# Attention scores as three fp32r passes over split queries and keys, in a two-layer diffusion backbone on one Trainium2 core

## The chip, the cores and the metric

One core of one Trainium2 chip runs the whole kernel. The metric is device time in microseconds (us) for one execution. The kernel before was timed three times: 1687.32, 1690.92 and 1691.16 us, with a median of 1690.92 us.

## What is computed

A context stream of 256 tokens and a latent stream of 256 tokens, each 1024 wide, go through two layers. A layer is a half-step feed-forward (SwiGLU, hidden width 2816), a mixer, and a second half-step feed-forward. The mixer holds attention next to a gated convolution and a multi-scale pooling, and projects all three back. The part that the change touches is the score product of the differential attention:

```python
def _diff_attn(q, k, v, lam):
    s = jnp.einsum('bqhid,bkhid->bhiqk', q, k, preferred_element_type=jnp.float32)
    p = jax.nn.softmax(s * (ATTN_HEAD_DIM ** -0.5), axis=-1)
    a = p[:, :, 0] - lam * p[:, :, 1]
    return jnp.einsum('bhqk,bkhe->bqhe', a.astype(v.dtype), v)
...
    q = _apply_rope(_rms(q.reshape(B, S, H, 2, dh), q_norm_w), cos, sin)
    k = _apply_rope(_rms(k.reshape(B, S, H, 2, dh), k_norm_w), cos, sin)
    k_all = jnp.concatenate([k, kc], axis=1)
```

There are 4 heads with 2 branches of 64 dimensions each. In layer 0 the latent queries see all 512 keys and the context queries see the 256 context keys. In layer 1 the context stream gives keys and values only.

## The kernel before

The activations lie transposed: 128 features on the partitions, tokens along the free dimension, 512 tokens (T) for both streams and 256 (S) for the latent one alone. The weights come as a stream of 320 blocks of 128x1024 numbers. SyncE loads block after block into a ring of 5 (`raw`). For each block ScalarE (ACT) writes a rounded fp32r copy (`whi`, `split` at L426 to L433), and VectorE (DVE) writes the rest (`wlo = raw - whi`, L761). TensorE (PE) then multiplies in three fp32r passes, high by high, high by low, low by high (`three`, L1287 to L1291). A block is 24 such matmuls. Every engine runs a list of instructions in a fixed order, written out by hand; semaphores tie the lists together. ACT and DVE issue their halves of block n+4 at the point where PE works on block n.

The mixer of a layer (`mixer(l)` on each engine) first makes 4 key blocks (b = 0 to 3, 512 tokens wide) and 4 query blocks (b = 4 to 7, 512 wide in layer 0, 256 wide in layer 1). This is called the query/key stage here. For each block b:

- PE does the 24 matmuls of the block, and then `stat(b-1)` (L1542), an fp32 matmul that sums squares for the RMS norm. `stat(c)` waits for the squares of block c (`sqk_done`) and for the exponentials of blocks up to c-2 (`rq_done`).
- ACT, in the loop that starts at L580, splits the weights of block b+4, copies block b out of PSUM into `kq` (L583), squares it (L586), and calls `lnexp(b-1)`: a logarithm into `lnk` (L572) and an exponential into `rq` (L577), which is the inverse root of the mean square.
- DVE, in the loop at L1107, makes `wlo` of block b+4 and calls `rope(b-1)` (L1075 to L1086): the norm's multiplication (L1079, which waits for `rq_done`), a shuffle, two products with cosine and sine, and a sum back into `kq`, which counts `qk_ready`.

After the eighth block PE waits for the sixth exponential (`pe.wait_ge(rq_done, 8 * l + 6)`) and starts the four value blocks, since these write the PSUM banks that the norm sums of blocks 4 and 5 were in. In between come the last `stat`, then a wait for all eight `qk_ready`, and the first two score units.

The attention runs in units (`units(l)`): one tile of 128 queries and one head against 512 keys (8 units in each layer), and in layer 0 four more units with one context tile and two heads against 256 keys. `scores(k)` (L1578 to L1590) makes the scores of a unit: for each head the two branches lie on partitions 0 to 63 and 64 to 127, and each is one fp32 matmul with 64 rows of contraction, into a PSUM bank of its own:

```python
ins = pe.matmul(ps[:, 2 * (u % 2) + b, j * wk:(j + 1) * wk],
                kq[rows, H + hd, t * P:(t + 1) * P], kq[rows, hd, T - wk:T],
                start=True, stop=True)
```

The unit's maximum is taken on DVE (`unit_max`, L1123), the exponential on ACT (`unit_exp`, L603), the difference of the two branches on DVE (`unit_dif`, L1132 to L1144), the transposes on PE (`turn`, L1602) and the product with the values on PE (`values`, L1620). Units 0 and 1 have their scores among the value blocks. The others are interleaved with 16 half blocks of the convolution and pooling projections, one unit for each half block. This is called the unit stage here.

Of the kernel before, what the change touches and what calls it, by code (L numbers as in the profile page):

```python
# [26 lines left out]
P = 128  # L27
# [7 lines left out]
H = 4  # L35
# [71 lines left out]
def program(nc, wstream, wmod, cols, x_t, out):  # L107
    with ExitStack() as ctx:
# [25 lines left out]

        shared_a = sb("shared_a", [P, 3 * T])
# [25 lines left out]
        wm0_place.close()  # L161
        kq = sb("kq", [P, 8, T])
        vt = sb("vt", [P, 4, T])
        cx = sb("cx", [P, 8, T])
# [67 lines left out]
        qk_ready = sem("qk_ready")  # L232
        score_done = sem("score_done")
# [32 lines left out]


# [48 lines left out]
        def ntile(l):  # L316
            return T if l == 0 else S
# [107 lines left out]
        def _(act):  # L425
# [134 lines left out]
            def mixer(l):  # L560
# [18 lines left out]

                for b in range(QKB):  # L580
                    split_next(n0 + b)
                    act.wait_ge(block_done, n0 + b + 1)
                    act.activation(kq[:, b, 0:wid(b)], ps[:, b % 4, 0:wid(b)], ACT.Copy).then_inc(evac, 1)  # L583
                    if b >= 2:
                        act.wait_ge(qk_stat, 8 * l + b - 1)
                    act.activation(sqk[:, b % 2, 0:wid(b)], ps[:, b % 4, 0:wid(b)], ACT.Square)\  # L586
                        .then_inc(sqk_done, 1)
                    if b >= 1:
                        lnexp(b - 1)
# [65 lines left out]
                split_next(n0 + VQ)  # L655
                lnexp(QKB - 1)
                split_next(n0 + VQ + 1)
                unit_exp(0)
# [90 lines left out]
        def _(dve):  # L749
# [337 lines left out]

            def lambda_sums():
# [17 lines left out]
            def mixer(l):  # L1106
                n0, w = B_win[l], ntile(l)  # L1107
                for b in range(QKB + 1):
                    split_next(n0 + b)
                    if b >= 1:  # L1110
                        rope(l, b - 1)

# [57 lines left out]
                split_next(n0 + VQ + 1)  # L1170
                unit_max(0)
# [114 lines left out]
        def _(pe):  # L1286
# [251 lines left out]
            def mixer(l):  # L1538
# [38 lines left out]
                def scores(k):  # L1577
# [4 lines left out]
                    if k >= 2:  # L1582

                        pe.wait_ge(exp_done, u - 1)
                    for j, hd in enumerate(hds):
                        for b in range(2):
                            rows = slice(DH * b, DH * b + DH)
                            ins = pe.matmul(ps[:, 2 * (u % 2) + b, j * wk:(j + 1) * wk],  # L1588
                                            kq[rows, H + hd, t * P:(t + 1) * P], kq[rows, hd, T - wk:T],
                                            start=True, stop=True)  # L1590
# [86 lines left out]
                pe.wait_ge(qk_ready, 8 * (l + 1))  # L1677
# [151 lines left out]
```

## Time and profile before

| what | value |
|---|---|
| median of three runs | 1690.92 us |
| the profiled execution's own time | 1691.61 us |
| its span | 1689.6 us |
| mean granted TensorE clock | 0.996 of full speed |
| TensorE busy (matmuls) | 1670.4 us, 99% |
| VectorE busy | 1099.2 us, 65% |
| ScalarE busy | 616.1 us, 36% |
| chain that ended last, by engine | PE 95%, DVE 2%, ACT 1%, issue 1%, DMA 1% |
| score matmuls (L1588) in that chain | 1% of the span |
| layer 0: query/key stage and value blocks | about 427 to 490 us from the span's start |
| layer 0: unit stage | about 490 to 560 us |
| layer 1: query/key stage | about 1376 to 1398 us |
| layer 1: value blocks, then unit stage | 1398 to 1424 us, then to about 1475 us |

A timeline row gives the start in us from the span's start, the length in us, the engine, the line, the operation, what is written and read, the shape and the number of instructions that were merged into the row. The last bracket, if there is one, is how long the engine had been idle and what ended that. PEld is TensorE's weight load, which can run beside its matmuls. An fp32 matmul of the program shows as two weight loads and two matmul records. The length of a record is longer than the distance to the next one on the same engine, since instructions overlap: the distance between starts is what an instruction costs in a dense stretch.

### The profile page before, as it was taken

To read this page: it belongs to the slowest core of one execution; us is meant where nothing else is said; L and a number is where in the kernel's file an instruction comes from. 1 tells how busy PE (TensorE), PEld (TensorE's weight loads), DVE (VectorE), ACT (ScalarE), POOL (GpSimd) and SP (SyncE) were. 2 spreads that over 40 slices of the span, in tenths; PEclk is the share of its full clock that TensorE was granted. 3 is DMA by queue.
4 is the path that set the end of the run, shared out by engine and by line. 5 is a ranking of instruction groups with operands and counts; after the bars stand their busy time and mean duration, and the time that the engine had idled before them with its cause. 6 is when DMAs were issued, how large, how long until landed. Compare 5 with 4: busy or idle time off the path is not lost.

```text
span 1689.6 us, 23906 instructions
## 1 busy us (share of the span) xinstructions
PE 1670.4 (99%) x9501; PEld 1411.1 (84%) x9501; DVE 1099.2 (65%) x1681; ACT 616.1 (36%) x948; POOL 84.7 (5%) x150
## 2 busy tenths in 40 slices
PE   7999999999999999999999999999999999999999
PEld 3788888889777898888878898888888897899999
DVE  4777777636668567787773377777723377876654
ACT  4422222124545443222222252222222265565542
POOL 0000000000000100101000000000000000100000
PEclk8999999999999999999999999999999999999999
DMA  9355555532211224555553224555422232255554
GB/s 370 116 190 181 195 179 192 182 112 76 94 68 51 80 86 159 181 193 184 190 176 124 87 101 162 192 183 191 158 100 93 81 110 91 89 189 186 179 183 150
DMA packets 69466, 249.42 MB, mean 148 GB/s; under 512 B 7536, under 2 KB 8560, under 8 KB 69360
## 3 DMA queue, kind: packets, MB, share of 16 engines
q1 hardware_dynamic: 50928, 180.82, 30.8%
q0 software_dynamic: 18432, 67.12, 11.8%
q8 instruction: 75, 1.23, 0.3%
q14 instruction: 31, 0.25, 0.0%
HBM read 246.86 MB, written 1.05 MB: 147 GB/s over the span
## 4 chain that ended last, share of the span: by engine, by line
PE 95%; DVE 2%; ACT 1%; issue 1%; DMA 1%; POOL 0%; POOLq 0%; ACTq 0%; DVEq 0%
PE ps L1289 30%; PE ps L1290 29%; PE ps L1291 29%; PE ps L1448 1%; PE ps L1588 1%; PE ps L1620 1%; PE ps L1548 1%; PE ps L1396 1%; ACT whi L432 0%; PE ps L1602 0%; DMA raw<-wstream 0%; DVE wlo L761 0%; PE ps L1424 0%; DVE nmax L1123 0%; PE ps L1463 0%
## 5 line engine op out<-in xcount | busy, mean ns | idle before, releaser
L761 DVE TENSOR_TENSOR wlo<-raw,whi 128x1024 fp32r<-128x1024 f32 x320 | 393.0, 1228 | 498.0 <-ACT whi L432 497.1
L432 ACT ACTIVATE whi<-raw 128x1024 fp32r<-128x1024 f32 x320 | 338.5, 1058 | 847.2 <-PE ps L1291 754.6
L1289 PE MATMUL ps<-xh,whi 128*128 128x512 f32 (+1 forms) x1580 | 585.9, 371 | 4.8 <-issue 2.0
L1290 PE MATMUL ps<-xl,whi 128*128 128x512 f32 (+1 forms) x1580 | 569.3, 360 | 0.0
L1291 PE MATMUL ps<-xh,wlo 128*128 128x512 f32 (+1 forms) x1580 | 568.8, 360 | 0.0
L1289 PEld LDWEIGHTS ps<-xh,whi 128*128 128x128 f32 x1580 | 298.3, 189 | 63.9 <-issue 16.7
L1290 PEld LDWEIGHTS ps<-xl,whi 128*128 128x128 f32 x1580 | 298.7, 189 | 46.8 <-issue 3.8
L1291 PEld LDWEIGHTS ps<-xh,wlo 128*128 128x128 f32 x1580 | 298.5, 189 | 45.3
L1289 PE MATMUL ps<-ah,whi 128*128 128x512 f32 (+2 forms) x976 | 324.3, 332 | 1.1 <-DVE shared_b L809 1.0
L1291 PE MATMUL ps<-ah,wlo 128*128 128x512 f32 (+2 forms) x976 | 322.2, 330 | 0.0
L786 DVE SCALAR_TENSOR_TENSOR shared_a<-wm,cs,shared_a 128x512 f32<-128x512 f32 x448 | 307.5, 745 | 0.0
L1290 PE MATMUL ps<-al,whi 128*128 128x512 f32 (+1 forms) x800 | 272.3, 340 | 0.0
L1289 PEld LDWEIGHTS ps<-ah,whi 128*128 128x128 f32 x976 | 184.8, 189 | 20.8 <-DVE shared_b L809 2.3
L1291 PEld LDWEIGHTS ps<-ah,wlo 128*128 128x128 f32 x976 | 184.9, 189 | 17.0
L1290 PEld LDWEIGHTS ps<-al,whi 128*128 128x128 f32 x800 | 151.7, 190 | 16.6
L390 POOL DMA_DIRECT2D wm<-wmod x126 | 66.5, 528 | 872.7 <-DVEq L789 865.1
L1290 PE MATMUL ps<-ah,whi 128*128 128x258 f32 x352 | 99.7, 283 | 0.0
L1290 PEld LDWEIGHTS ps<-ah,whi 128*128 128x128 f32 x352 | 66.9, 190 | 0.0
L828 DVE SCALAR_TENSOR_TENSOR h<-ps,gcol,h 128x256 f32<-128x256 f32 x104 | 45.6, 477 | 22.8 <-PE ps L1291 22.7
L522 ACT ACTIVATE shared_a<-h 128x256 f32<-128x256 f32 (+1 forms) x64 | 31.4, 496 | 62.5 <-DVE h L828 59.9
L1289 PE MATMUL ps<-al,whi 128*128 128x256 f32 x176 | 49.8, 283 | 0.0
L1291 PE MATMUL ps<-al,wlo 128*128 128x256 f32 x176 | 49.8, 283 | 0.0
(128 smaller groups left out, 1106.1 us busy)
## 6 DMA issues: line engine op xcount, KB each, us to landing
raw<-wstream SPq DMA_DIRECT2D x320, 512.0 KB, 3.5
wm<-wmod POOLq DMA_DIRECT2D x128, 512.0 KB, 4.6
wm<-wmod SPq DMA_DIRECT2D x8, 1024.0 KB, 17.6
h<-x_t SPq DMA_DIRECT2D x4, 512.0 KB, 6.6
out_t<-h SPq DMA_DIRECT2D x8, 128.0 KB, 2.6
K<-cols SPq DMA_DIRECT2D x1, 939.0 KB, 20.1
K<-cols SPq DMA_DIRECT2D x1, 265.5 KB, 2.7
lamk<-cols SPq DMA_DIRECT2D x1, 256.0 KB, 16.5
```

Of the source, the lines that this page charges most:

```text
L390: pool.dma_start(wm[:, c, :, :].rearrange("p a n -> p (a n)"), wmod[bass.ds(i * 2 + c, 1)].rearrange("a p n -> p (a n)"))\
L432: act.activation(whi[:, n % SPL, :, :].rearrange("p a b -> p (a b)"), raw[:, n % RING, :], ACT.Copy)\
L522: act.activation(sq[:, d % 2, a:b], h[:, d, a:b], ACT.Square).then_inc(sq_done, 1)
L761: dve.tensor_tensor(wlo[:, n % RING, :, :].rearrange("p a b -> p (a b)"), raw[:, n % RING, :], whi[:, n % SPL, :, :].rearrange("p a b -> p ...
L786: ins = dve.scalar_tensor_tensor(acc, src, sc, acc, ALU.mult, ALU.add)
L828: ins = dve.scalar_tensor_tensor(h[:, d, v * S:(v + 1) * S], ps[:, bank, v * S:(v + 1) * S], gcol[:, m, d, v:v + 1], h[:, d, v * S:(v + 1) ...
L1289: pe.matmul(out_ap, hi_w, hi_x, start=start, stop=False)
L1290: pe.matmul(out_ap, hi_w, lo_x, start=False, stop=False)
L1291: return pe.matmul(out_ap, lo_w, hi_x, start=False, stop=stop)
L1396: ins = pe.matmul(ps[32 * g:32 * g + 2, ROWS_BANKS[d % 2], 0:w], cs[:, 2 * c:2 * c + 2], wm0[:, d, c // 4, g * w:(g + 1) * w], start=c < 4 ...
L1448: ins = pe.matmul(ps[32 * j:32 * j + 32, ROWS_BANK, 0:P], col("pick", 31 - r, 32), macc[:, v, j * P:(j + 1) * P], start=r == 0, stop=u + 1 ...
L1548: pe.matmul(ps[:, stat_bank(b), 0:wb], col("halves", 0, P), sqk[:, b % 2, 0:wb], start=True, stop=True)\
```

## The change

The scores are no longer fp32 products. After `rope(b)`, ACT writes a rounded fp32r copy of `kq[:, b]` (`head_high`), and DVE overwrites `kq[:, b]` with the rest (`head_low`; `kql` is the same memory as `kq`, with the type fp32r). The copies lie in memory that is free in this stage: `kh` and `qh` over `shared_a` and `shared_b`, the last one over a part of `cx`. Each score product becomes three fp32r matmuls that add up in PSUM. The wait of PE for all eight `qk_ready` goes away; instead `scores` waits for the low half of its own query head, and the first one also for the last logarithm.

```diff
--- before.py
+++ after.py
@@ -132,6 +132,10 @@
         qws = sb("qws", [P, 16])
         mrows = sb("mrows", [P, P])
 
+        heads = ExitStack()
+        qh = heads.enter_context(nc.sbuf_tensor("qh", [P, 3, T], F32R))
+        kh = heads.enter_context(nc.sbuf_tensor("kh", [P, 4, T], F32R))
+        heads.close()
         shared_a = sb("shared_a", [P, 3 * T])
         macc = shared_a[:, 0:2 * HN].rearrange("p (v n) -> p v n", v=2)
         sq = shared_a[:, 0:2 * T].rearrange("p (a t) -> p a t", a=2)
@@ -159,8 +163,15 @@
         lamk = wm0_place.enter_context(nc.sbuf_tensor("lamk", [P, NLAM], F32))
         lamt = wm0_place.enter_context(nc.sbuf_tensor("lamt", [P, 2, DH], F32))
         wm0_place.close()
+        heads_low = ExitStack()
+        kql = heads_low.enter_context(nc.sbuf_tensor("kql", [P, 8, T], F32R))
+        heads_low.close()
         kq = sb("kq", [P, 8, T])
         vt = sb("vt", [P, 4, T])
+        fifth = ExitStack()
+        fifth.enter_context(nc.sbuf_tensor("five", [P, 5, T], F32))
+        qh_last = fifth.enter_context(nc.sbuf_tensor("qh_last", [P, T], F32R))
+        fifth.close()
         cx = sb("cx", [P, 8, T])
         sqk = sb("sqk", [P, 2, T])
         lnk = sb("lnk", [P, T])
@@ -230,6 +241,8 @@
         rq_done = sem("rq_done")
         qk_used = sem("qk_used")
         qk_ready = sem("qk_ready")
+        kq_hi = sem("kq_hi")
+        kq_lo = sem("kq_lo")
         score_done = sem("score_done")
         max_done = sem("max_done")
         exp_done = sem("exp_done")
@@ -265,6 +278,9 @@
         srow_done = sem("srow_done")
 
 
+        def kq_high(b):
+            return kh[:, b, :] if b < 4 else qh[:, b - 4, :] if b < 7 else qh_last[:, :]
+
         def width(m):
             return T if m < 5 else S
 
@@ -577,6 +593,11 @@
                     act.activation(rq[:, c % 2, 0:wid(c)], lnk[:, 0:wid(c)], ACT.Exp, scale=-0.5)\
                         .then_inc(rq_done, 1)
 
+                def head_high(b):
+
+                    act.wait_ge(qk_ready, 8 * l + b + 1)
+                    act.activation(kq_high(b)[:, 0:wid(b)], kq[:, b, 0:wid(b)], ACT.Copy).then_inc(kq_hi, 1)
+
                 for b in range(QKB):
                     split_next(n0 + b)
                     act.wait_ge(block_done, n0 + b + 1)
@@ -585,6 +606,8 @@
                         act.wait_ge(qk_stat, 8 * l + b - 1)
                     act.activation(sqk[:, b % 2, 0:wid(b)], ps[:, b % 4, 0:wid(b)], ACT.Square)\
                         .then_inc(sqk_done, 1)
+                    if b >= 2:
+                        head_high(b - 2)
                     if b >= 1:
                         lnexp(b - 1)
 
@@ -653,8 +676,10 @@
                     act.activation(xh[:, 0:H, t * P:(t + 1) * P], of[:, t, :, :], ACT.Copy).then_inc(yh_done, 1)
 
                 split_next(n0 + VQ)
+                head_high(QKB - 2)
                 lnexp(QKB - 1)
                 split_next(n0 + VQ + 1)
+                head_high(QKB - 1)
                 unit_exp(0)
                 split_next(n0 + VQ + 2)
                 unit_exp(1)
@@ -1085,6 +1110,13 @@
                 own(dve.tensor_tensor(rot[:, :], shf[:, :], col("sin", 0, S), ALU.mult))
                 dve.tensor_tensor(kq[:, b, 0:S], kq[:, b, 0:S], rot[:, :], ALU.add).then_inc(qk_ready, 1)
 
+            def head_low(l, b):
+
+                wb = T if b < 4 else ntile(l)
+                dve.wait_ge(kq_hi, 8 * l + b + 1)
+                dve.tensor_tensor(kql[:, b, 0:wb], kq[:, b, 0:wb], kq_high(b)[:, 0:wb].bitcast(F32),
+                                  ALU.subtract).then_inc(kq_lo, 1)
+
             def lambda_sums():
 
                 for l in range(DEPTH):
@@ -1109,6 +1141,8 @@
                     split_next(n0 + b)
                     if b >= 1:
                         rope(l, b - 1)
+                    if b >= 2:
+                        head_low(l, b - 2)
 
                 us = units(l)
 
@@ -1168,6 +1202,7 @@
                         .then_inc(yl_done, 1)
 
                 split_next(n0 + VQ + 1)
+                head_low(l, QKB - 1)
                 unit_max(0)
                 split_next(n0 + VQ + 2)
                 unit_max(1)
@@ -1582,12 +1617,19 @@
                     if k >= 2:
 
                         pe.wait_ge(exp_done, u - 1)
+                    if k == 0:
+
+                        pe.wait_ge(lnk_done, 8 * (l + 1))
+                    pe.wait_ge(kq_lo, 8 * l + H + hds[-1] + 1)
                     for j, hd in enumerate(hds):
-                        for b in range(2):
-                            rows = slice(DH * b, DH * b + DH)
-                            ins = pe.matmul(ps[:, 2 * (u % 2) + b, j * wk:(j + 1) * wk],
-                                            kq[rows, H + hd, t * P:(t + 1) * P], kq[rows, hd, T - wk:T],
-                                            start=True, stop=True)
+                        q_hi, k_hi = kq_high(H + hd), kq_high(hd)
+                        q_lo, k_lo = kql[:, H + hd, :], kql[:, hd, :]
+                        for i, (q, k_) in enumerate(((q_hi, k_hi), (q_hi, k_lo), (q_lo, k_hi))):
+                            for b in range(2):
+                                rows = slice(DH * b, DH * b + DH)
+                                ins = pe.matmul(ps[:, 2 * (u % 2) + b, j * wk:(j + 1) * wk],
+                                                q[rows, t * P:(t + 1) * P], k_[rows, T - wk:T],
+                                                start=i == 0, stop=i == 2)
                     ins.then_inc(score_done, 1)
 
                 def turn(k):
@@ -1674,7 +1716,6 @@
                 value_block(0)
                 stat(QKB - 1)
                 value_block(1)
-                pe.wait_ge(qk_ready, 8 * (l + 1))
                 scores(0)
                 value_block(2)
                 scores(1)
```

The instruction lists show where the new operations stand. In each list L-numbers are those of that version. First ScalarE in the query/key stage of layer 1, at b = 4, before:

```order
L432 ACTIVATE whi<-raw 128x1024 [waits block_done,raw_in4]
L583 ACTIVATE kq<-ps 128x256 [waits block_done]
L586 ACTIVATE sqk<-ps 128x256 [waits qk_stat]
L572 ACTIVATE lnk<-ps,K 128x512 [waits rq_done,qk_stat]
L577 ACTIVATE rq<-lnk 128x512 [waits qk_used,lnk_done]
```

and after the change (`kh<-kq` is `head_high`):

```order
L448 ACTIVATE whi<-raw 128x1024 [waits block_done,raw_in4]
L604 ACTIVATE kq<-ps 128x256 [waits block_done]
L607 ACTIVATE sqk<-ps 128x256 [waits qk_stat]
L599 ACTIVATE kh<-kq 128x512 [waits qk_ready]
L588 ACTIVATE lnk<-ps,K 128x512 [waits rq_done,qk_stat]
L593 ACTIVATE rq<-lnk 128x512 [waits qk_used,lnk_done]
```

Between the square of block b and the logarithm of block b-1 there is now a copy of block b-2, which waits for `qk_ready`, the end of DVE's `rope(b-2)`. The logarithm behind it waits with it.

Then VectorE in the same stage, at b = 3, before:

```order
L761 TENSOR_TENSOR wlo<-raw,whi 128x1024 [waits hi_done]
L1079 SCALAR_TENSOR_TENSOR kq<-kq,K,rq 128x512 [waits rq_done]
L1083 STREAM_SHUFFLE shf<-kq 128x256 [waits qk_used]
L1084 TENSOR_TENSOR kq<-kq,K 128x256 [waits dve_step]
L1085 TENSOR_TENSOR rot<-shf,K 128x256
L1086 TENSOR_TENSOR kq<-kq,rot 128x256 [waits dve_step]
```

and after the change (`kql<-kq,kh` is `head_low`):

```order
L786 TENSOR_TENSOR wlo<-raw,whi 128x1024 [waits hi_done]
L1104 SCALAR_TENSOR_TENSOR kq<-kq,K,rq 128x512 [waits rq_done]
L1108 STREAM_SHUFFLE shf<-kq 128x256 [waits qk_used]
L1109 TENSOR_TENSOR kq<-kq,K 128x256 [waits dve_step]
L1110 TENSOR_TENSOR rot<-shf,K 128x256
L1111 TENSOR_TENSOR kq<-kq,rot 128x256 [waits dve_step]
L1117 TENSOR_TENSOR kql<-kq,kh 128x512 [waits kq_hi]
```

The subtraction of block b-2 now stands between the sum that ends `rope(b-1)` and the next weights.

Last, TensorE at the second score unit of layer 0, at the end of a value block and the start of the next, before:

```order
L1291 MATMUL ps<-whi,xl 128x512
L1588 MATMUL ps<-kq 128x512 x2
L1289 MATMUL ps<-whi,xh 128x512 [waits lo_done]
L1290 MATMUL ps<-wlo,xh 128x512
L1291 MATMUL ps<-whi,xl 128x512
```

and after the change:

```order
L1326 MATMUL ps<-whi,xl 128x512
L1630 MATMUL ps<-kh,qh 128x512 [waits kq_lo]
L1630 MATMUL ps<-kh,qh 128x512
L1630 MATMUL ps<-kql,qh 128x512 x2
L1630 MATMUL ps<-kh,kql 128x512 x2
L1324 MATMUL ps<-whi,xh 128x512 [waits lo_done]
L1325 MATMUL ps<-wlo,xh 128x512
L1326 MATMUL ps<-whi,xl 128x512
```

Two fp32 matmuls became six fp32r matmuls, in three pairs; the two of a pair use partitions 0 to 63 and 64 to 127.

## Rows read from the trace of the kernel before

**Rows 1.** Waits of TensorE over the whole span: total us, times, longest us.

```profile
PE ps L1620 <- DVE of L1154: 1.7, 1, 1.7
```

**Rows 2.** Timeline, first score unit of layer 0: start us, length us.

```profile
475.08 0.30 PEld L1588 LDWEIGHTS ps<-kq 64*128 64x128 f32 x4 [0.35 <-issue]
475.08 0.70 PE L1588 MATMUL ps<-kq 64*128 64x512 f32 x2
...
475.08 1.13 PE L1588 MATMUL ps<-kq 64*128 64x512 f32 x4
476.14 0.50 PE L1289 MATMUL ps<-whi,xh 128*128 128x512 f32 x1
```

**Rows 3.** Timeline, first unit of layer 0 with two heads (TensorE).

```profile
518.99 0.49 PE L1588 MATMUL ps<-kq 64*128 64x256 f32 x2
...
518.99 0.70 PE L1588 MATMUL ps<-kq 64*128 64x256 f32 x4
...
520.05 0.33 PE L1602 MATMUL ps<-K,att 128*128 128x128 f32 x1
```

**Rows 4.** Timeline, TensorE, last key and query blocks of layer 1.

```profile
1394.75 0.59 PE L1548 MATMUL ps<-sqk,K 128*128 128x256 f32 x2
...
1398.05 0.59 PE L1548 MATMUL ps<-sqk,K 128*128 128x256 f32 x2
1398.29 0.58 PE L1289 MATMUL ps<-whi,xh 128*128 128x512 f32 x1
...
1409.95 0.70 PE L1588 MATMUL ps<-kq 64*128 64x512 f32 x2
```

**Rows 5.** Timeline, ScalarE (ACT), query/key stage of layer 1.

```profile
1386.39 0.58 ACT L583 ACTIVATE kq<-ps 128x512 f32<-128x512 f32 x1
...
1387.35 0.69 ACT L572 ACTIVATE lnk<-ps,K 128x512 f32<-128x512 f32 x1
1388.07 0.63 ACT L577 ACTIVATE rq<-lnk 128x512 f32<-128x512 f32 x1
1388.60 1.04 ACT L432 ACTIVATE whi<-raw 128x1024 fp32r<-128x1024 f32 x1
1389.55 0.36 ACT L583 ACTIVATE kq<-ps 128x256 f32<-128x256 f32 x1
...
1396.62 0.48 ACT L572 ACTIVATE lnk<-ps,K 128x256 f32<-128x256 f32 x1
1397.13 0.42 ACT L577 ACTIVATE rq<-lnk 128x256 f32<-128x256 f32 x1
```

**Rows 6.** Timeline, VectorE (DVE), the same stage.

```profile
1385.58 0.75 DVE L1079 SCALAR_TENSOR_TENSOR kq<-kq,K,rq 128x512 f32<-128x512 f32 x1 [1.34 <-ACT rq L577]
...
1387.99 1.22 DVE L761 TENSOR_TENSOR wlo<-raw,whi 128x1024 fp32r<-128x1024 f32 x1
1389.12 0.75 DVE L1079 SCALAR_TENSOR_TENSOR kq<-kq,K,rq 128x512 f32<-128x512 f32 x1
...
1396.20 0.48 DVE L1079 SCALAR_TENSOR_TENSOR kq<-kq,qws,rq 128x256 f32<-128x256 f32 x1
...
1398.34 1.22 DVE L761 TENSOR_TENSOR wlo<-raw,whi 128x1024 fp32r<-128x1024 f32 x1
```

**Rows 7.** Groups by form that stand nearest to the added operations.

```profile
L817 DVE TENSOR_TENSOR al<-shared_b,ah 128x512 fp32r<-128x512 f32 x66 | 45.2, 684 | 1.0 <-ACT ah L451 0.7
...
L451 ACT ACTIVATE ah<-shared_b 128x512 fp32r<-128x512 f32 x66 | 40.6, 615 | 4.2 <-DVE shared_b L809 4.2
...
L817 DVE TENSOR_TENSOR al<-shared_b,al 128x256 fp32r<-128x256 f32 x22 | 9.2, 419 | 0.5 <-ACT al L451 0.5
L451 ACT ACTIVATE al<-shared_b 128x256 fp32r<-128x256 f32 x22 | 8.9, 403 | 1.4 <-DVE shared_b L997 1.3
```

**Rows 8.** Waits of VectorE from 1424 to 1448 us.

```profile
DVE nmax L1123 <- PE ps L1588: 2.8, 1, 2.8
```

**Rows 9.** Layer 1 stretches; PE, PEld, DVE, ACT, POOL busy us, then granted clock.

```profile
1448.00:1475.00 27.00, 24.80 (x196) 23.41 (x195) 21.77 (x37) 16.19 (x30) 4.27 (x4) 1.00 0.30 102
```

## The prediction

> **What bounds the kernel now.** I read the waits of TensorE (PE) first. Over the whole span it waits for other engines in very few places; the largest is 1.7 us for VectorE (DVE) in the unit stage of layer 1 [rows 1], and none lies in the mixer of layer 0. So nearly every us that PE's own work gains or loses in the mixer of layer 0 moves the end one for one, and work on ScalarE (ACT) and DVE is free as long as PE does not come to wait for it. Then I read the timeline of the score units, to price a score product, and last the timelines of the query/key stage of layer 1, where PE's steps are shortest and the other two engines have the least room. A change of 0.3%, about 5 us here, is about what a measurement of this kernel can tell from no change.
>
> **Score units on PE.** An fp32 matmul is two records. In the first unit of layer 0 the first pair of records (one for each branch) ends 0.70 us after the start, both pairs end after 1.13 us: one step is 0.43 us for 512 columns, and the two branches run side by side on their halves of the partitions, since two records share one step [rows 2]. The next work starts 1.06 us after the unit's start [rows 2], so the unit is 2 x 0.43 plus 0.20 us for getting in and out. A unit with two heads, 256 columns, ends its first pair after 0.49 us and its second after 0.70: a step of 0.21 us, four of them and the same 0.2 make the 1.06 us from 518.99 to 520.05 [rows 3].
>
> What does an fp32r pair cost? No row shows one with 64 rows of contraction. The fp32 step of 256 columns streams each column twice in its 0.21 us, as much as one fp32r pass over 512 columns would; and its pair of weight loads is as large as the new one and is hidden under that step, since the steps come 0.21 us apart [rows 3]. So I take 0.21 us for a pair of 512 and, for a pair of 256, half a step, 0.11 us. A 512 unit becomes 3 x 0.21 + 0.20 = 0.83 us, 0.23 less than 1.06; I take 0.21 less, for a little more per instruction. A two-head unit becomes 6 x 0.11 + 0.20 = 0.86 us; I take 0.15 less than 1.06, since its weight loads have only half as long to hide in. The bounds: nothing is gained if the loads are not hidden, and 0.4 us per unit is lost if the branches do not run side by side (both under the rivals).
>
> Which units count? In layer 0 all: 8 x 0.21 + 4 x 0.15 = 2.3 us. In layer 1 the first three: scores 0, 1 and 2 are in the path, and at unit 2 DVE waits 2.8 us for PE [rows 8]. From there on DVE has no other wait for PE until 1448 us [rows 8], and it is PE that then waits 1.7 us for DVE [rows 1]. A faster PE only waits longer there, so units 3 to 7 gain nothing. That is 3 x 0.21 = 0.6 us. Sum of the gain: 2.9 us.
>
> **New work on ACT and DVE: 16 copies and 16 subtractions.** The nearest forms are the same operations on the hidden values: copy 615 ns at 512 and 403 ns at 256 columns, subtraction 684 and 419 ns [rows 7]. On both engines the next instruction starts some 0.1 us before the record of the last one ends (in rows 5 the copy and the square of 0.58 and 0.59 us take 0.96 us together; in rows 6 the 1.22 us weight subtraction at 1387.99 is followed at 1389.12). So I charge 0.51 and 0.30 us for a copy, 0.59 and 0.34 for a subtraction.
>
> In layer 0 all eight blocks are 512 wide, PE takes over 6 us for each (24 matmuls of about 0.23 and a norm sum), and what ACT and DVE add, 1.1 us a block, has its cover. The same holds for the value blocks, 5.83 us each (two of them lie between 1398.29 and 1409.95) [rows 4].
>
> In layer 1 a query block is 256 wide and a block with its norm sum takes 3.30 us (1394.75 to 1398.05) [rows 4]. DVE needs 1.13 + 2.14 = 3.27 us for each (the weight subtraction, and the rope from 1396.20 to 1398.34) [rows 6]; it had no room. Worse, a ring of waits now ties the two engines: the logarithm of block b-1 stands behind the copy of b-2, which waits for the end of rope(b-2), and rope(b-1) waits for the exponential. Step by step, with a rope of 512 columns 2.41 us (1385.58 to 1387.99) and ready 0.08 later, of 256 columns 2.14 and 0.08 [rows 6]; logarithm and exponential of 512 together 1.25 us to the next instruction (1387.35 to 1388.60), of 256 about 0.84, and the exponential's end 0.09 later [rows 5]:
>
> - rope(1) is ready at 1388.07, as before. The copy of block 1 runs to 1388.6; before, the logarithm of block 2 began at 1387.35. Its exponential ends at 1390.0, and rope(2) starts there, not at 1389.12.
> - rope(2) is ready at 1392.5, the copy ends at 1393.0, the exponential of block 3 at 1394.4, rope(3) starts there and is ready at 1396.9. DVE meanwhile does the subtractions.
> - ACT ends that round at 1394.3. Its split (0.94 us) and the copy of block 5 (0.27) then put the square of block 5 at 1395.5 to 1395.9. PE wanted it at 1394.75 for its norm sum [rows 4]: **1.2 us of waiting**.
> - The copy of block 3 starts at 1397.0, the exponential of block 4 ends at 1398.4. DVE, with low(2) (0.59) and the weights (1.13) behind rope(3), starts rope(4) at 1398.6 (before 1396.20 [rows 6]), ready at 1400.8.
> - The next split puts the square of block 6 at 1399.5 to 1399.9; PE, shifted by 1.2, wanted it at 1399.25: **0.7 us more**.
> - The copy of block 4 (0.30) starts at 1400.8, the exponential of block 5 ends at 1402.1, where it ended at 1397.55 [rows 5]. The first value block waits for it. It started at 1398.29 [rows 4] and now starts at 1402.1: **1.9 us more**, 3.85 us in all.
>
> Behind it nothing adds: the value blocks give both engines 5.83 us each. By the same steps the last rope is ready at 1412.5 and the first unit's maximum starts 0.3 us later than PE's shift explains, with a value block between it and the next score that waits for it. The first score needs the last logarithm (about 1409.8) and low(4) (1405), and comes at 1413.8. PE's shift stays: DVE's chain from unit 2 on is released by PE [rows 8].
>
> The price of the stall has its ends too. It is nothing if the rounds overlap better than I have them, and if each added operation of blocks 0 to 5 stood in the path it would be 4 x (0.51 + 0.59) + 2 x (0.30 + 0.34) = 5.7 us. I take the worked-out 3.85, from the rows at the place itself.
>
> **Sum.** 1691.61 (the profiled execution) + 3.85 - 2.9 = 1692.5 us. The median of the runs shown is 1690.92, 0.7 below the profiled one. The forecast is no change that can be told.
>
> **The rivals.**
>
> Loads that are not hidden. If each new pair shows its weight loads, a pair costs more by half of the 0.20 us of getting in and out [rows 2], 0.10 us. A 512 unit is then 3 x 0.21 + 0.20 + 2 x 0.10 = 1.03 us, no gain worth naming, and a two-head unit 6 x 0.11 + 0.20 + 5 x 0.10 = 1.36, 0.30 more: 3.85 - 0.3 + 1.2 = 4.7, so 1696.3 us. It decides from 0.05 us a pair. Against it speak the 0.21 us steps of [rows 3], where loads into the same rows were hidden. The Trainium skill ("TensorE: Matmul & The Clock Gate", Part 3: Packing small matmuls) says that a weight load overlaps a running matmul only where the row group differs; by that rule it would come out as this rival, and the rows disagree with it for fp32. Chance 0.08.
>
> Branches that do not run side by side (**slower**). Then a 512 unit has six passes of 0.21 and costs 1.46, 0.4 more, and a two-head unit 12 x 0.11 + 0.20 = 1.52, 0.46 more: 11 x 0.4 + 4 x 0.46 = 6.2 us, and 0.3 more in layer 1 where five units lose 2.0 us and only 1.7 is spare. With the stall 10.4: 1702.0 us. Against it: the shared steps of [rows 2]. For it: no fp32r pair is in the trace. It decides once a pair takes over 0.30 us. Chance 0.12.
>
> A stall that costs more: PE idle for 3.85 us within 8, and the granted clock, 1.00 also where PE was busy 24.8 of 27 us [rows 9], falls to the lower level. If the first value block ran at 1.2 GHz in place of 2.4, it would take up to 5.8 us more, so 1698.3 us. Chance 0.09. Against it: the stall comes in three parts with norm sums and a query block between them.
>
> No stall: ACT and DVE keep up after all. Then 1691.61 - 2.9 = 1688.7 us. It wants an ACT round that doesn't wait for rope. The order of the lists speaks against it. Chance 0.13. That the products stay fp32 is ruled out by the types in the list of the changed program; that they gain far more than 0.21 has no source, 0.03.
>
> **How the numbers follow.** The forecast has a chance of 0.55, with 1690.5 to 1695 as its own range, for stalls of 2 to 6 us. The range takes in the case without a stall, the loads that are not hidden and the loss of the clock: 1688.3 to 1698.3, and leaves out mainly the branches one after the other. Faster by over 0.3% (under 1685.9) takes more than all the gains together: 0.04. Slower by over 0.3% (over 1696.0) is 0.12 from the branches, 0.05 from the loads and 0.07 from the clock: 0.24. Within 0.3%: 0.72.
>
> **What the next profile would show.** Right: PE waits for a square (ACT) before the norm sums of blocks 5 and 6 of layer 1, and for an exponential before the first value block, 3 to 5 us together; score units of about 0.85 us; the wait for the attention output (L1154 in the version before) grown from 1.7 to some 2.7 us; nothing new in layer 0. Wrong: score units over 1.06 us, a value block in layer 1 that starts on time, or a granted clock of half after 1395 us.

## The result, and the profile after the change

| | before | after |
|---|---|---|
| median | 1690.01 us (18 runs, 1685.18 to 1692.07) | 1692.62 us (18 runs, 1689.90 to 1695.70) |
| profiled execution: span | 1689.6 us | 1693.5 us |
| profiled execution: mean granted clock | 0.996 | 0.995 |

The ratio is 1.0018, with a 95% interval from 1.0011 to 1.0025: some 3 us slower, within the 0.3% that was called no change, and close to the 1692.5 us of the forecast. Both are given over all executions; the three of before that stand ahead of the prediction are among its 18.

The waits of TensorE over the whole execution of the changed kernel have two large entries that the kernel before did not have, for an exponential and for squares of ScalarE, and the wait of [rows 1] has grown (a third new entry in the mixer, for VectorE's difference of a unit, is 0.2 us):

```profile
PE ps L1662 <- DVE of L1188: 2.1, 1, 2.1
...
PE ps L1324 <- ACT rq L593: 1.5, 1, 1.5
PE ps L1583 <- ACT sqk L607: 1.3, 2, 0.9
```

The timeline of TensorE shows them in layer 1. First a row from ahead of any of these waits, the norm sums of blocks 1 and 2, in the kernel before and in the changed one:

```profile
1383.13 0.59 PE L1548 MATMUL ps<-sqk,K 128*128 128x512 f32 x1
...
1380.09 0.59 PE L1583 MATMUL ps<-sqk,K 128*128 128x512 f32 x1
```

Then the norm sum of block 5, which comes after a wait ([rows 4] before):

```profile
1392.91 0.70 PE L1583 MATMUL ps<-sqk,K 128*128 128x256 f32 x2 [0.87 <-ACT sqk L607]
```

And the norm sum of block 6 and the first value block, each after a wait:

```profile
1396.91 0.70 PE L1583 MATMUL ps<-sqk,K 128*128 128x256 f32 x2 [0.43 <-ACT sqk L607]
1399.06 0.50 PE L1324 MATMUL ps<-whi,xh 128*128 128x512 f32 x1 [1.46 <-ACT rq L593]
1399.40 0.42 PE L1325 MATMUL ps<-wlo,xh 128*128 128x512 f32 x1
1399.64 0.61 PE L1326 MATMUL ps<-whi,xl 128*128 128x512 f32 x1
1400.04 0.63 PE L1324 MATMUL ps<-whi,xh 128*128 128x512 f32 x1
1400.47 0.63 PE L1325 MATMUL ps<-wlo,xh 128*128 128x512 f32 x1
```

At the norm sums of blocks 1 and 2 the two executions are 3.04 us apart (1383.13 - 1380.09). Against that distance the norm sum of block 5 is late by 1.20 us (1392.91 + 3.04 - 1394.75), that of block 6 by 1.90 (1396.91 + 3.04 - 1398.05) and the value block by 3.81 (1399.06 + 3.04 - 1398.29). The profile names less than that as waiting: the three idle times add up to 0.87 + 0.43 + 1.46 = 2.8 us. So the delay is read here from the starts of the same instruction in both kernels, and the list of waits only says where to look. The last rows show something else: from 1400.0 on the matmuls of the value block start 0.43 us apart, where a step is 0.23 us at full clock. The windows of the same execution show the granted clock there and in one more place, and in the stretch between:

```profile
1396.00:1399.60 3.60, 1.72 (x9) 1.06 (x8) 3.49 (x9) 2.65 (x7) 0.00 (x0) 1.00 0.42 146
1399.60:1403.00 3.40, 3.40 (x9) 2.62 (x8) 3.29 (x9) 2.10 (x6) 0.00 (x0) 0.51 0.00 0
1403.00:1448.00 45.00, 44.16 (x267) 35.34 (x265) 32.84 (x62) 22.49 (x49) 1.05 (x2) 1.00 0.23 74
1450.80:1454.20 3.40, 3.40 (x19) 3.40 (x18) 2.49 (x6) 2.06 (x4) 0.00 (x0) 0.51 0.00 0
```

The columns are the stretch, its length, then busy time and instructions of PE, PEld, DVE, ACT and POOL (GpSimd), the granted clock (1.00 is 2.4 GHz, 0.5 is 1.2 GHz) and the DMA engines' share and GB/s. The first fall comes after the three waits, the second after the wait for the attention output, 2.1 us long (1.7 us in the kernel before, where the clock held).

The ring of waits that the prediction worked out (exponential behind copy, copy behind rope, rope behind exponential) can be read in the timeline of ScalarE, round b = 4 of layer 1. ScalarE stood idle for 1.07 us until the rope of block 2 ended, then came its copy, and logarithm and exponential of block 3 behind it ([rows 5] before):

```profile
1386.84 1.04 ACT L448 ACTIVATE whi<-raw 128x1024 fp32r<-128x1024 f32 x1
1387.79 0.37 ACT L604 ACTIVATE kq<-ps 128x256 f32<-128x256 f32 x1
1388.05 0.38 ACT L607 ACTIVATE sqk<-ps 128x256 f32<-128x256 f32 x1
1389.49 0.63 ACT L599 ACTIVATE kh<-kq 128x512 fp32r<-128x512 f32 x1 [1.07 <-DVE kq L1111]
1390.03 0.67 ACT L588 ACTIVATE lnk<-ps,K 128x512 f32<-128x512 f32 x1
1390.73 0.63 ACT L593 ACTIVATE rq<-lnk 128x512 f32<-128x512 f32 x1
```

The score units: the timeline of TensorE at the first unit of layer 0 ([rows 2] before):

```profile
474.06 0.50 PE L1630 MATMUL ps<-kh,qh 64*128 64x512 f32 x2
474.40 0.40 PE L1630 MATMUL ps<-kql,qh 64*128 64x512 f32 x2
474.63 0.40 PE L1630 MATMUL ps<-kh,kql 64*128 64x512 f32 x2
474.96 0.50 PE L1324 MATMUL ps<-whi,xh 128*128 128x512 f32 x1
```

And at the first unit with two heads ([rows 3] before):

```profile
516.63 0.38 PE L1630 MATMUL ps<-kh,qh 64*128 64x256 f32 x2
516.85 0.28 PE L1630 MATMUL ps<-kql,qh 64*128 64x256 f32 x2
516.97 0.28 PE L1630 MATMUL ps<-kh,kql 64*128 64x256 f32 x2
...
517.53 0.33 PE L1644 MATMUL ps<-K,att 128*128 128x128 f32 x1
```

A 512 unit takes 0.90 us in place of 1.06, in three pairs; the two matmuls of a pair run side by side (one step for two records). A two-head unit takes 0.90 in place of 1.06 too, in six pairs 0.12 us apart within a head. Over a longer stretch the saving is read more finely: the first unit started 1.02 us earlier than in the kernel before (474.06 against 475.08), the norm sums in layer 1 3.04 us earlier, so the twelve units of layer 0 saved 2.02 us, 0.168 us each. In the mixer of layer 0 TensorE waits for no other engine.

### The profile page after: what moved, and what is told of

It reads as the page before. It is cut to its first block, busy times and chain, and to the rows that moved or that the text cites. A ratio compares the mean times of both kernels' runs of the same rounds, so it can differ in the third digit from the quotient of the medians.

```text
span 1693.5 us, 24052 instructions
## 1 busy us (share of the span) xinstructions
PE 1670.2 (99%) x9549; PEld 1416.1 (84%) x9549; DVE 1108.1 (65%) x1697; ACT 624.5 (37%) x964; POOL 84.7 (5%) x150
## 4 chain that ended last, share of the span: by engine, by line
PE 94%; DVE 3%; ACT 1%; issue 1%; DMA 0%; POOLq 0%; POOL 0%; ACTq 0%; DVEq 0%
PE ps L1324 30%; PE ps L1325 29%; PE ps L1326 29%; PE ps L1483 1%; PE ps L1662 1%; PE ps L1630 1%; DVE wlo L786 1%; ACT whi L448 1%; PE ps L1583 1%; PE ps L1644 0%; PE ps L1431 0%; PE ps L1459 0%; DVE nmax L1157 0%; PE ps L1498 0%; PE ps L1500 0%
```

## The experiments

Each ran beside the kernel before on the same chip, with its executions compared to that kernel's. Executions of one kernel differ in their mean granted clock, in the profiled ones mostly by what happens in the first 35 us, and within every kernel the time follows it: 1.2 to 1.4 us for each 0.001. So two numbers are given for each run below: the mean of the granted clock over its executions, and the time at equal clock, read at 0.998 from a line through its own executions. Over its 89 executions beside the experiments the kernel before has a mean clock of 0.9983 and 1689.3 us at equal clock (0.9981 to 0.9985 and 1689.2 to 1689.4 in the three rounds of measurement).

| run | executions | ratio to before (95%) | at equal clock, against before | mean clock |
|---|---|---|---|---|
| the change (first time) | 18 | 1.0018 (1.0011 to 1.0025) | +1.4 | 0.9966 |
| a2_after_again | 11 | 1.0018 (1.0009 to 1.0027) | +1.2 | 0.9966 |
| s1_splits_only | 12 | 1.0026 (1.0016 to 1.0037) | +3.4 | 0.9976 |
| f3_scores_only | 11 | 0.9991 (0.9980 to 1.0001) | -2.2 | 0.9977 |
| e1_copy_after_exp | 11 | 0.9999 (0.9990 to 1.0009) | -1.8 | 0.9973 |
| e2_copy_one_later | 11 | 0.9999 (0.9989 to 1.0010) | -2.4 | 0.9969 |
| h1_layer0_only | 12 | 0.9992 (0.9982 to 1.0002) | -1.4 | 0.9983 |
| t1_tile_out_act | 11 | 0.9978 (0.9969 to 0.9987) | -3.1 | 0.9985 |
| t0_before_tile_out | 12 | 0.9993 (0.9984 to 1.0001) | -0.4 | 0.9985 |
| p1_low_on_pool | 6 | 1.0038 (1.0024 to 1.0051) | +2.5 | 0.9955 |
| c1_longer_wait | 12 | 1.0007 (0.9999 to 1.0016) | +0.6 | 0.9978 |
| f1_one_pass | 5 | 0.9962 (0.9949 to 0.9975) | -8.4 | 0.9964 |

The standard error of the third number (the time at equal clock) is 0.1 to 0.4 us (0.5 for a2, 1.1 for f1), that of a mean clock 0.0002 to 0.0006.

**Splits alone, and scores alone.** The first takes the new copies and subtractions, and leaves the scores as they were; the second does the opposite.

```diff
 # s1_splits_only, against after
-                dve.tensor_tensor(kql[:, b, 0:wb], kq[:, b, 0:wb], kq_high(b)[:, 0:wb].bitcast(F32),
+                dve.tensor_tensor(att[:, b % 3, 0:wb].bitcast(F32R), kq[:, b, 0:wb], kq_high(b)[:, 0:wb].bitcast(F32),
                                   ALU.subtract).then_inc(kq_lo, 1)
...
 # f3_scores_only, against before
...
-                        for b in range(2):
...
+                        q_hi, k_hi, q_lo, k_lo = xh[:, H + hd, :], xh[:, hd, :], xl[:, H + hd, :], xl[:, hd, :]
+                        for i, (q, k_) in enumerate(((q_hi, k_hi), (q_hi, k_lo), (q_lo, k_hi))):
+                            for b in range(2):
...
```

> The kernel before, with the 16 copies on ScalarE and the 16 subtractions on VectorE put where the change has them, and the scores left as fp32 products (the low halves are written to the memory of att and never used). Theory A (the cost is the ring of waits in the query/key stage of layer 1, and the score products are a separate gain): TensorE waits about 3.3 us there as after the change, score units stay at 1.06 us, and the time is the one before plus 3.4 us, plus 0 to 2 us where the granted clock falls. Theory B (the cost comes with the new score products, by the clock or by their weight loads): no change against before.

> The kernel before, with the scores as three fp32r passes, but on data that is there anyway (xh and xl in place of split queries and keys, so the attention works on other numbers), and no copies or subtractions. Theory A: units of 0.895 us in place of 1.06, 15 of them count, so 2.5 us faster than before (1687.5 us against 1690.0), no wait in the query/key stage and a granted clock that stays up. Theory B: no gain, or the clock falls in the mixer of layer 1 here too.

The two parts add up at equal clock: +3.4 and -2.2 make +1.2, and the change has +1.2 to +1.4 at equal clock. The two new waits for ScalarE in s1 are those of the changed kernel, with fp32 scores, its first value block is 3.8 us late too, and its wait for the attention output is the 1.7 us of [rows 1]:

```profile
PE ps L1658 <- DVE of L1188: 1.7, 1, 1.7
PE ps L1324 <- ACT rq L593: 1.5, 1, 1.5
PE ps L1583 <- ACT sqk L607: 1.3, 2, 0.9
```

So the waits come from the splits, and theory B is out for them. But f3 also lost clock (0.9977, and in its profiled execution a fall right after the wait for the attention output, which is 2.1 us there too), which theory A had not expected: the gain of 2.2 us shows in the median as 1.7. The 3.3 us of TensorE's waits that the expectations start from are 2.8 us in the list of waits and 3.8 us of delay; their 2.0 and 2.4 us for the attention output are 1.7 and 2.1 us in the list.

**Where the copy stands, and who subtracts.** e1 only swaps two calls (in the loop, and once more behind it); e2 also moves both parts by one round; p1 leaves the order of the change and gives the subtraction to GpSimd.

```diff
 # e1_copy_after_exp
-                    if b >= 2:
-                        head_high(b - 2)
                     if b >= 1:
                         lnexp(b - 1)
+                    if b >= 2:
+                        head_high(b - 2)
...
 # e2_copy_one_later, on ScalarE; head_low moves in the same way on VectorE
...
+                    if b >= 3:
+                        head_high(b - 3)
...
 # p1_low_on_pool, on GpSimd; both calls of head_low on VectorE are gone
+                for b in range(QKB):
+                    wb = T if b < 4 else ntile(l)
+                    pool.wait_ge(kq_hi, 8 * l + b + 1)
+                    pool.tensor_tensor(kql[:, b, 0:wb], kq[:, b, 0:wb], kq_high(b)[:, 0:wb].bitcast(F32),
+                                       ALU.subtract).then_inc(kq_lo, 1)
```

> After the change, with the copy of block b-2 behind the logarithm and exponential of block b-1 instead of in front of them. Theory A (ring of waits): the exponential no longer waits for the rope of the block before, and of the 3.3 us of TensorE's waits about 1 us is left; 2.3 us faster than after the change. Theory C (VectorE has simply too much work, 3.6 to 3.9 us a block against 3.3): the waits stay near 3.3 us and the time too.

> As the run with the copy behind the exponential, and both copy and subtraction one block later (block b-3 in round b). Theory A: no rope is waited for by ScalarE, so TensorE's waits before the first value block fall to under 0.3 us, the granted clock stays up, and the time is that before minus 2.5 us (about 1687.5 us). Theory C: VectorE's load is the same, the waits stay near 3 us.

> After the change, with the 16 subtractions on GpSimd (1.65 us at 512 columns there) in place of VectorE. Theory A (ring: exponential waits for copy, copy for rope, rope for exponential): the ring turns as slowly as before, TensorE's waits stay at 2.7 us or more of the 3.3. Theory C (VectorE's load): without the 0.34 to 0.59 us a block VectorE keeps up and the waits fall under 1 us.

The swap takes away most of the stall. The waits of e1 in the mixer of layer 1 show no wait for ScalarE any more:

```profile
PE ps L1662 <- DVE of L1188: 2.1, 1, 2.1
PE ps L1324 <- POOL xl L427: 1.7, 2, 1.5
PE ps L1644 <- DVE att L1178: 0.2, 1, 0.2
```

But the starts show that a part is left, as expected: measured as above from the norm sums of blocks 1 and 2 (1379.97 in e1), the first value block starts at 1396.20 and is 1.1 us late (1396.20 + 3.16 - 1398.29), in place of 3.8. The reason is in the timeline of ScalarE. The exponential is ahead of the copy now, but the copy of block 3 still waits for its rope, and behind it come the next weights, the squares of block 6 and the exponential of block 5, which ends at 1396.15, just ahead of the value block:

```profile
1393.22 0.63 ACT L599 ACTIVATE kh<-kq 128x512 fp32r<-128x512 f32 x1 [1.09 <-DVE kq L1111]
```

In e2 the copy comes a round later, and the first value block is on time to 0.01 us (norm sums at 1377.74, value block at 1392.89). VectorE is busy there for 26.5 of the 28 us from 1381.65 on, and TensorE works through all 28. So VectorE's load alone (theory C) does not cost TensorE anything; the ring does. At equal clock e1 is 0.6 us behind e2, with errors of 0.2 each: the direction of the 1.1 us, if not all of it. What was expected of e2's clock did not come: it fell here too.

p1 leaves the ring as it is and takes the subtractions from VectorE. That makes less work there (22.6 us busy from 1384 to 1412 us, 24.1 in the changed kernel), yet the waits are longer, and the first value block is 4.5 us late:

```profile
PE ps L1327 <- ACT rq L599: 1.9, 1, 1.9
...
PE ps L1586 <- ACT sqk L613: 1.6, 2, 1.0
```

Why longer is in the forms of VectorE from 1384 to 1412 us in p1: the rope's first operation, which has three inputs and is a part of the ring, takes 862 ns; the two-input operations of the rope take what they took:

```profile
L1110 DVE SCALAR_TENSOR_TENSOR kq<-kq,qws,rq 128x256 f32<-128x256 f32 x4 | 3.4, 862 | 0.7 <-ACT rq L599 0.7
L1115 DVE TENSOR_TENSOR kq<-kq,K 128x256 f32<-128x256 f32 x7 | 3.0, 426 | 0.2
```

The same operation in the same stretch of the changed kernel takes 477 ns:

```profile
L1104 DVE SCALAR_TENSOR_TENSOR kq<-kq,qws,rq 128x256 f32<-128x256 f32 x4 | 1.9, 477 | 0.0
```

The timeline of p1 shows what it ran beside. All four times it started while GpSimd's subtraction was under way, and it ended 0.28 us (once 0.29) after that one; two of the four:

```profile
1394.86 1.55 POOL L420 TENSOR_TENSOR kql<-kq,kh 128x512 fp32r<-128x512 f32 x1 [3.02 <-ACT kh L605]
1395.63 1.06 DVE L1110 SCALAR_TENSOR_TENSOR kq<-kq,qws,rq 128x256 f32<-128x256 f32 x1 [0.38 <-ACT rq L599]
...
1398.95 1.20 POOL L420 TENSOR_TENSOR kql<-kq,qh 128x256 fp32r<-128x256 f32 x1 [2.54 <-ACT qh L605]
1399.72 0.72 DVE L1110 SCALAR_TENSOR_TENSOR kq<-kq,qws,rq 128x256 f32<-128x256 f32 x1 [0.16 <-ACT rq L599]
```

The rope's other operations all ran after GpSimd was done, so their unchanged times say nothing on this. And since p1 lengthens a part of the ring, it does not separate the theories by itself; e1 and e2 do.

**The clock and the length of TensorE's waits.** With e1 and e2 the change is 1.8 and 2.4 us faster than before at equal clock, yet as fast as before in the ratio, since their clock is lower. Four runs ask what lowers it, and the change ran once more beside them. h1 applies the change in layer 0 only; t1 is e2 with the copy of the attention output moved from VectorE to ScalarE; t0 is the kernel before with that move; c1 is the kernel before with one more VectorE operation ahead of that copy in layer 1.

```diff
 # t0_before_tile_out and t1_tile_out_act, on ScalarE; tile_out(t) is gone on VectorE
+                        if p == e + 2:
+                            act.wait_ge(pv_done, U0[l] + e + 1)
+                            act.activation(of[:, t, :, :], ps[:, 4, :].rearrange("p (h q) -> p h q", h=H), ACT.Copy)\
+                                .then_inc(of_done, 1)
...
 # c1_longer_wait, on VectorE, at p == e + 2
+                            if l == 1 and t == 0:
+                                own(dve.tensor_tensor(rot[:, :], shf[:, :], col("cos", 0, S), ALU.mult))
                             tile_out(t)
```

> The change in layer 0 only; layer 1 keeps fp32 scores and has no copies or subtractions. Theory A (in layer 0 the splits are free and TensorE's gain counts whole; the costs are all in layer 1: 3.3 us of waits, and a clock that falls because a faster TensorE waits longer there): 12 units at 0.165 us give 2.0 us, mean granted clock as before (0.9985), so 2.0 us faster than before. Theory D (the lower clock comes with fp32r scores as such): the clock's mean falls to about 0.997 and the gain shrinks below 0.5 us.

> The run with copy and subtraction one block later, and in addition the copy of the attention output out of PSUM (0.68 us, for which TensorE waits 2.4 us in the unit stage of layer 1) on ScalarE in place of VectorE. Theory A (the long wait of TensorE in layer 1 is what lets the granted clock fall): no single wait there over 1.3 us, the mean clock back at 0.998 or more, about 1.0 to 1.5 us faster than the run without it. Theory D: the clock stays near 0.997 and the gain is at most the 0.6 us that VectorE is relieved of.

> Control: the kernel before with that same copy on ScalarE and nothing else. Theory A: the wait of 2.0 us of TensorE in layer 1 shrinks by about 1 us, which is also what the time gains at most; the clock's mean rises slightly above 0.9985. Theory D: the same without the clock.

> The kernel before, fp32 scores and no splits, with one more VectorE operation (256 columns, 0.4 us, result unused) ahead of the copy of the attention output in layer 1, so that TensorE's one wait of 2.0 us there becomes 2.4 us, as long as it is with fp32r scores. Theory A (the length of that wait sets how often the granted clock falls): mean clock falls from 0.9983 to about 0.997, and the time rises by 0.4 us plus 1.5 to 2 us. Theory D (fp32r scores in layer 1 are what lowers it): clock as before, 0.4 us slower.

> The changed kernel once more, beside the others. Theory A: 1.0 us slower than before at equal clock and a mean clock of 0.9966, 2.5 to 3.5 us slower in all.

h1 keeps its clock and gains 1.4 us at equal clock, less than the 2.0 of its units by two errors. t0 gains 0.4, less than the 1 us that was possible, and its clock is that of before within the error. a2 repeats the first measurement. In t1 TensorE's waits in the unit stage of layer 1 are at most 1.0 us, and its clock is back at 0.9985 (the 1.5 us for GpSimd in the first line lie behind the unit stage, where e1, f3 and the changed kernel have them too):

```profile
PE ps L1327 <- POOL xl L427: 1.7, 2, 1.5
PE ps L1327 <- DVE cx L1097: 1.0, 1, 1.0
PE ps L1647 <- DVE att L1183: 0.7, 2, 0.4
```

Against e2 it gained 0.6 us at equal clock, and with the clock 0.0021 in the ratio, 3.5 us, more than twice the 1.0 to 1.5 us that was expected. It has fp32r scores in both layers, so these do not lower the clock by themselves. In c1 the scores are fp32 and the wait is 2.2 us; its profiled execution shows the clock fall behind that wait:

```profile
1439.00:1442.70 3.70, 1.62 (x14) 1.38 (x13) 3.56 (x7) 1.04 (x3) 0.00 (x0) 0.99 0.40 107
1442.70:1446.10 3.40, 3.27 (x15) 3.31 (x16) 2.91 (x7) 2.63 (x6) 0.00 (x0) 0.51 0.11 42
```

In h1 TensorE waits 1.7 us and the clock stays at 1.00 in the stretch that follows:

```profile
1442.70:1446.10 3.40, 3.40 (x30) 3.40 (x31) 2.45 (x7) 3.33 (x8) 0.00 (x0) 1.00 0.15 59
```

Over all profiled executions: of the eight in which TensorE waits 2.1 or 2.2 us for the attention output (after, a2, e1, e2, f3, f1, p1, c1) the clock fell behind that wait in all but p1; in the three with 1.7 us (before, s1, h1) and the two with waits of at most 1.0 us (t0, t1) it did not fall. Behind the stall in the query/key stage it fell in two of the four profiled executions that have the stall (after and p1, not a2 and s1). The mean clock of c1, 0.9978 with an error of 0.0003, against 0.9981 in the same round and 0.9983 over all, is a much smaller loss than expected and inside its error. So c1 shows one fall behind a longer wait with fp32 scores; that the length of this wait alone sets how often the clock falls stays open. That the lower mean clocks come from these falls is also only seen in the profiled executions: the others have a mean clock and nothing on where it fell.

**The price of a pass.** f1 is f3 with the second and third pass left out.

```diff
 # f1_one_pass, against f3_scores_only; stop is set with the first pass
-                        for i, (q, k_) in enumerate(((q_hi, k_hi), (q_hi, k_lo), (q_lo, k_hi))):
+                        for i, (q, k_) in enumerate(((q_hi, k_hi),)):
```

> The kernel before with scores of a single fp32r pass over other data (xh), two of the three passes left out, no splits. Price of a pair of passes from the unit of 0.895 us: 0.235 us, so a unit takes 0.43 us. 15 units that count gain 0.63 us each: 9.4 us at equal clock against before (1679.5 us). In layer 1 TensorE's waits for VectorE grow by 5 times 0.47 us against the three-pass run, to 4.5 us or more, and by theory A the clock falls at least as often as there (mean 0.9975 or less). If passes overlap with the loads of the half blocks, the gain is smaller, 7 us.

A unit takes 0.43 us, so a pair of matmuls (one pass of both branches) costs 0.23 us, in the changed kernel and here. At equal clock 8.4 of the 9.4 us arrive, with an error of 1.1; TensorE now waits in a few more places, up to 0.8 us for an exponential and 1.0 us for the difference on VectorE. Its waits for VectorE in layer 1 are 2.1 and 1.0 us and not the 4.5 that were expected. The median shows 5.7, the clock being 0.9964.

## Why the prediction was right, and where it was off

- **What bounds it.** Right. TensorE's gain in layer 0 counts (h1: 1.4 +- 0.3 us at equal clock for 2.0 us less work; the trace of the changed kernel shows the whole 2.0), and the splits there cost nothing. In layer 1 the units from number 3 on gain nothing: from the start of unit 2 to the end of the wait for VectorE it is 24.30 us before (1423.43 to 1447.73) and 24.12 after (1425.37 to 1449.49), which is what unit 2 alone saves. The wait named grew only from 1.7 to 2.1 us (forecast: 2.7), with 0.2 us of a new one for VectorE ahead of it and smaller savings than forecast.
- **The score units.** The mechanism was right, both rivals about it are out: the loads are hidden (the 256-column pairs start 0.12 us apart) and the branches run side by side. The rule of the Trainium skill ("TensorE: Matmul & The Clock Gate", Part 3: Packing small matmuls), that a weight load overlaps a running matmul only where the row group differs, does not hold here either: each of those pairs loads into the rows of the pair before, with load records of 0.18 us. The term was mis-sized: a 512 unit saves 0.17 us and not 0.21, since a pair takes 0.23 and not 0.21 us; a two-head unit saves 0.16 to 0.18 (0.15 was forecast). With the 0.168 us of the long stretch, 15 units make 2.5 us in place of 2.9; f3 shows 2.2 at equal clock.
- **The stall.** It lies where it was worked out, at the squares of blocks 5 and 6 and the exponential of block 5, and has the forecast size as a delay: 1.20, 0.70 and 1.91 us for 1.2, 0.7 and 1.9, and 3.81 for 3.85 in all. As waits the profile was to show 3 to 5 us, and it shows 2.8. s1 costs 3.4 us at equal clock, a little over one error of 0.3 less. The reason was right as well: e1, which only swaps the two calls, has 1.1 us of it left, and e2, in which ScalarE waits for no rope, has none, with VectorE busier than in the changed kernel. "Behind it nothing adds" held too.
- **The clock.** This was a rival with a chance of 0.09, at one place and with 5.8 us. It is part of the result: the mean clock fell from 0.9983 to 0.9966, at 1.3 us for 0.001 some 2.2 us. The prediction itself gave "a granted clock of half after 1395 us" as a sign of being wrong, and in the profiled execution it came in two places: behind the stall, as the rival had it, and behind the wait for the attention output in the unit stage, which the prediction named as growing, "only waits longer there", and priced at nothing. That is the step that was wrong, in an otherwise right account. Each fall lasted 3.4 us at half clock in work without gaps, some 1.7 us, where the rival had priced a whole value block. With fp32 scores (s1) the clock held behind the stall in the one profiled execution, and it was 0.9976 +- 0.0005 on average, so how much of the loss belongs to which of the two places is not shown.
- **The sum.** 3.8 - 2.5 = 1.3 us of steps, 1.2 to 1.4 measured at equal clock, plus 2.2 of clock: 3.5 us, for a measured ratio of 1.0018, 3.0 us (1.9 to 4.2). The clock of before is that of the other rounds here; its 18 executions beside the change have none on record. The forecast was 0.9 us above the profiled execution of before, so the change was forecast as 0.9 us and measured as 3.0. That the two medians agree to 0.1 us is mostly luck: the forecast started from the 1691.61 us of that execution, the median of before is 1.6 us under it, and the clock cost about as much as this start was too high.

A version that beats both kernels came out of this: t1, with copy and subtraction a round later and the attention output copied by ScalarE, has a median of 1685.11 us, a ratio of 0.9978 (0.9969 to 0.9987) to the kernel before.

## What to carry to other kernels

When work is put into an engine's list in front of something that another engine waits for, look for the ring: here a copy that needed rope(b-2) stood ahead of the exponential that rope(b-1) needed. The swap of two calls took away 2.7 us of a delay of 3.8, and moving the copy a round later the rest. Read a delay from the starts of the same instruction in both kernels: e1 was 1.1 us late with no wait for ScalarE in its list. A gain on the engine that bounds is worth nothing in a stretch where it waits for another engine, and here the longer wait mostly went along with a lower granted clock behind it. Where executions differ by as much as the effect, read the time against each execution's mean granted clock before calling two versions the same.

## What was not expected of the hardware

- Time against clock: within each kernel that was timed, 0.001 of mean granted clock goes with 1.2 to 1.4 us.
- Behind a wait of 2.1 or 2.2 us for the attention output, seven of eight profiled executions had TensorE at 1.2 GHz for a stretch; with 1.7 us or less there, none of five. Behind the stall of the changed kernel, at the same clock, the steps of the value block are 0.43 us in place of 0.23.
- With a subtraction on GpSimd under way when it started, VectorE's three-input operation of 256 columns took 862 ns on average in place of 477 and ended 0.28 us after GpSimd's work. Two-input operations are not exempt as such: VectorE's weight subtraction kept its 1.22 us beside GpSimd's work at 1398.34 us of p1, but took 1.65 us beside GpSimd's subtraction at 1471.63 us of the changed kernel.
